# Mixture-of-experts stage: seven of the eight experts in one TensorE loop, fed from a fixed copy of their queue

## What is computed

```python
def _swiglu(x, w1, w3, w2):
    return (jax.nn.silu(x @ w1) * (x @ w3)) @ w2

def _moe(x, w_router, w1, w3, w2):
    logits = (xt @ w_router).astype(jnp.float32)
    top_v, top_e = lax.top_k(logits, TOP_K)          # TOP_K = 2 of N_EXPERTS = 8
    gates = jax.nn.softmax(top_v, axis=-1)
    ...                                              # sort the tokens by expert
    yb = lax.map(run, ...)                           # run: _swiglu(xb, w1[e], w3[e], w2[e])
    y = jnp.zeros((T, D), x.dtype).at[stok].add(yb[dest] * sg[:, None])
```

## Time and profile before

| | us |
|---|---|
| median of 3 runs | 2779.47 (2777.61 to 2779.65) |
| the profiled execution, its own time | 2774.82 |
| its span in the profile | 2773.0 |
| TensorE busy | 2689.7 (97% of the span) |
| experts' up steps, 14336 matmul records | 617.9 busy |
| experts' down steps, 7168 matmul records | 321.1 busy |
| first matmul of expert 0 | at 1828.61 |

### The profile page before, as it was taken

How to read it: one execution, slowest core, us unless ns; L and a number is a source line. 1 busy time by engine, 2 the same in 40 slices (tenths; PEclk the granted TensorE clock), 3 DMA queues, 4 the chain that set the end, 5 groups by cost and what they waited for, 6 DMA issues and landing times.

```text
span 2773.0 us, 73042 instructions
## 1 busy us (share of the span) xinstructions
PE 2689.7 (97%) x33424; PEld 2268.6 (82%) x33424; DVE 890.5 (32%) x1659; ACT 365.2 (13%) x829; POOL 19.6 (1%) x36
## 2 busy tenths in 40 slices
PE   7999999899999999999999999999999999999998
PEld 6877678887667768857877788589999999999997
DVE  5441454623697333444443334410000000000002
ACT  1002241210100023300001242110000000000000
POOL 0000000000000000000000000000000000000000
PEclk9999999999999999999999999999999999999999
DMA  5434232013434434333445242459999999999996
GB/s 198 182 136 184 107 149 85 4 55 137 150 136 158 178 123 152 125 121 139 180 155 196 108 156 107 152 213 391 382 370 398 379 401 373 383 402 373 395 386 256
DMA packets 55718, 601.57 MB, mean 217 GB/s; under 512 B 6337, under 2 KB 6465, under 8 KB 10129
## 3 DMA queue, kind: packets, MB, share of 16 engines
q1 hardware_dynamic: 52272, 587.74, 54.0%
q0 software_dynamic: 3296, 11.57, 1.1%
HBM read 595.48 MB, written 3.81 MB: 216 GB/s over the span
## 4 chain that ended last, share of the span: by engine, by line
PE 91%; DMA 4%; DVE 3%; issue 1%; ACT 1%; POOL 0%; SPq 0%; DVEq 0%; POOLq 0%; ACTq 0%
PE bank L311 21%; PE bank L2511 19%; PE bank L443 10%; PE bank L2523 9%; PE bank L475 8%; PE bank L321 6%; PE bank L464 4%; DMA slot<-in_experts 4%; PE bank L1642 3%; PE bank L1208 2%; PE bank L1628 1%; DVE arena L1833 1%; PE bank L2563 1%; PE bank L936 1%; PE bank L1229 1%
## 5 line engine op out<-in xcount | busy, mean ns | idle before, releaser
L2511 PE MATMUL bank<-arena,slot 128*64 128x96 f32 x14336 | 617.9, 246 | 11.4 <-issue 8.3
L2511 PEld LDWEIGHTS bank<-arena,slot 128*64 128x64 f32 x14336 | 603.2, 137 | 16.3 <-issue 16.0
L311 PE MATMUL bank<-h_cm,slot 128*128 128x256 f32 (+2 forms) x2032 | 448.3, 382 | 1.1 <-ACT h_cm L350 0.5
L311 PEld LDWEIGHTS bank<-h_cm,slot 128*128 128x128 f32 (+2 forms) x2032 | 383.4, 190 | 64.1 <-issue 9.6
L2523 PE MATMUL bank<-ff,slot 128*64 128x96 f32 x7168 | 321.1, 246 | 11.5 <-DMA slot<-in_experts 7.5
L2523 PEld LDWEIGHTS bank<-ff,slot 128*64 128x64 f32 x7168 | 307.7, 137 | 13.7 <-issue 13.6
L2680 DVE TENSOR_TENSOR ff<-ff,bank 128x192 f32<-128x192 f32 x112 | 39.7, 355 | 798.6 <-PE bank L2511 798.6
L475 PE MATMUL bank<-slot,ff 128*128 128x512 f32 x528 | 231.6, 592 | 1.8 <-DVE ff L608 1.8
L475 PEld LDWEIGHTS bank<-slot,ff 128*128 128x128 f32 x528 | 98.7, 190 | 114.6 <-issue 111.9
L464 PE MATMUL bank<-h_cm,slot 128*128 128x256 f32 x704 | 153.6, 379 | 0.4 <-ACT h_cm L352 0.4
L464 PEld LDWEIGHTS bank<-h_cm,slot 128*128 128x128 f32 x704 | 133.7, 190 | 22.5 <-issue 4.9
(11 more groups left out here) (403 smaller groups left out, 2013.9 us busy)
## 6 DMA issues: line engine op xcount, KB each, us to landing
slot<-in_experts SPq DMA_DIRECT2D x112, 2048.0 KB, 9.1
slot<-in_experts SPq DMA_DIRECT2D x112, 1024.0 KB, 9.1
slot<-in_ffn SPq DMA_DIRECT2D x22, 2048.0 KB, 9.3
slot<-in_ffn SPq DMA_DIRECT2D x22, 1024.0 KB, 5.0
slot<-in_dense SPq DMA_DIRECT2D x11, 2048.0 KB, 9.3
slot<-in_dqk SPq DMA_DIRECT2D x8, 2048.0 KB, 8.0
slot<-in_g SPq DMA_DIRECT2D x8, 2048.0 KB, 8.0
slot<-in_w_in_rkv SPq DMA_DIRECT2D x6, 2048.0 KB, 7.7
```

The lines of the kernel that those rows point to most:

```text
L311: ins = pe.matmul(ps[0:m, j * S:(j + 1) * S], w[:, k * width + c0:k * width + c0 + m], rhs[:, k, :], start=k == 0, stop=k == ks - 1)
L2511: ins = pe.matmul(bank[64 * c:64 * c + 64, m * PLACES:(m + 1) * PLACES], slot[s][:, c0:c0 + 64], QUEUE[:, e, k, :], start=k == 0, stop=k = ...
```

## The change

Expert 0 stays written out. Experts 1 to 7 are one engine loop on TensorE with the loop of six rounds inside it. For that, every address in the loop must be the same for each expert: DVE copies the queue of the next expert to a fixed place, CURRENT (128 x 768 f32), and TensorE reads it from there and waits for a new semaphore, current_ready. The sums are always in banks 4 and 5, and the transposes always in 6 and 7. Before down 0 TensorE now waits until banks 4 and 5 have been copied out (sums_read of the expert before), and before the transposes until banks 6 and 7 have been (sums_ready; it has one more count, given once by two tiny copies at the start). ACT, DVE, SP and POOL stay written out as they were.

```diff
+        CURRENT = arena[:, 21248:21248 + KD * PLACES].rearrange("p (k s) -> p k s", s=PLACES)
...
-                                            QUEUE[:, e, k, :], start=k == 0, stop=k == KD - 1, skip_group_check=True)
+                                            CURRENT[:, k, :], start=k == 0, stop=k == KD - 1, skip_group_check=True)
...
-                        ins = pe.matmul(PS[down_bank(e) + d // 4][64 * c:64 * c + 64, (d % 4) * PLACES:(d % 4 + 1) * PLACES],
+                        ins = pe.matmul(PS[4 + d // 4][64 * c:64 * c + 64, (d % 4) * PLACES:(d % 4 + 1) * PLACES],
...
             for half in range(2):
                 pe.wait_ge(sums_read[half], p * N_EXPERTS + e + 1)
+                pe.wait_ge(sums_ready[half], p * (N_EXPERTS + 1) + e + 1)
                 for d in range(4):
-                    ins = pe.transpose(PS[down_bank(e) + half][0:PLACES, d * P:(d + 1) * P], Y_CM[half][:, d, :], ident)
+                    ins = pe.transpose(PS[6 + half][0:PLACES, d * P:(d + 1) * P], Y_CM[half][:, d, :], ident)
...
-                for e in range(N_EXPERTS):
+
+                def expert(e, turn):
                     first = p * ALL_UNITS + e * U_EXPERT + n0
...
+                    pe.wait_ge(named("current_ready"), p * N_EXPERTS + e + 1)
                     up(0, 0)
                     up(0, 1)
-                    if e >= 2:
+                    if turn:
                         for half in range(2):
-                            pe.wait_ge(sums_ready[half], p * N_EXPERTS + e - 1)
+                            pe.wait_ge(sums_read[half], p * N_EXPERTS + e)
                     down(0, 0, start=True)
-                    if e:
+                    if turn:
                         pe_moe_turn(pe, p, e - 1)
                     with pe.Fori(0, U_EXPERT // 2 - 1) as i:
...
+                expert(0, False)
+                with pe.Fori(1, N_EXPERTS) as e:
+                    expert(e, True)
                 pe_moe_turn(pe, p, N_EXPERTS - 1)
...
+                act.copy(stat[:, 13:14], ident[:, 0:1]).then_inc(sums_ready[0], 1)
...
+                def current(e):
+                    if e:
+                        dve.wait_ge(up_ready, p * ALL_UNITS + e * U_EXPERT + n0)
+                    else:
+                        for b in range(2):
+                            dve.wait_ge(named(f"moe_bank_read{b}"), p * moe_reads(b) + moe_reads(b))
+                    v.tensor_copy(CURRENT, QUEUE[:, e]).then_inc(named("current_ready"), 1)
...
+                v.tensor_copy(stat[:, 15:16], ident[:, 0:1]).then_inc(sums_ready[1], 1)
+                current(0)
                 dve.wait_ge(named("places_moved"), p + 1)
                 dve_rows(dve, p)
...
+                    if e < LAST:
+                        current(e + 1)
                     moe_down(dve, p, e, 1, v.tensor_copy)
```

More of the change, by code:

```diff
@@ L2498, in moe_reads, with pe_moe_unit_up @@
             return (GATHERS + TURNED + 1 - b) // 2
-        def pe_moe_unit_up(pe, par, e, n, loads, s):
+        def pe_moe_unit_up(pe, par, n, loads, s):
             pe.wait_ge(slot_loaded[s], 16 * loads)
@@ L2511, in pe_moe_unit_up, with pe_moe_unit_down @@
                             ins = pe.matmul(bank[64 * c:64 * c + 64, m * PLACES:(m + 1) * PLACES], slot[s][:, c0:c0 + 64],
-                                            QUEUE[:, e, k, :], start=k == 0, stop=k == KD - 1, skip_group_check=True)
+                                            CURRENT[:, k, :], start=k == 0, stop=k == KD - 1, skip_group_check=True)
                 ins.then_inc(ready, 1)
-        def pe_moe_unit_down(pe, par, e, n, loads, s, start=False, stop=False):
+        def pe_moe_unit_down(pe, par, n, loads, s, start=False, stop=False):
             pe.wait_ge(slot_loaded[s], 16 * loads)
@@ L2527, in pe_moe_unit_down @@
             ins.then_inc(down_done, 1)
-        def down_bank(e):
-            return 4 + 2 * (e % 2)
         def pe_moe_turn(pe, p, e):
@@ L2577, in up @@
                         at = L + 2 * j
-                        pe_moe_unit_up(pe, (n0 + j) % 2, e, first + j + 2 * i, first_round + (at // SLOTS + 1) + i,
-                                       at % SLOTS)
+                        pe_moe_unit_up(pe, (n0 + j) % 2, first + j + 2 * i, first_round + (at // SLOTS + 1) + i, at % SLOTS)
                     def down(i, j, **kw):
                         at = L + 2 * j + 1
-                        pe_moe_unit_down(pe, (n0 + j) % 2, e, first + j + 2 * i, first_round + (at // SLOTS + 1) + i,
+                        pe_moe_unit_down(pe, (n0 + j) % 2, first + j + 2 * i, first_round + (at // SLOTS + 1) + i,
                                          at % SLOTS, **kw)
+                    pe.wait_ge(named("current_ready"), p * N_EXPERTS + e + 1)
                     up(0, 0)
                     up(0, 1)
-                    if e >= 2:
+                    if turn:
                         for half in range(2):
-                            pe.wait_ge(sums_ready[half], p * N_EXPERTS + e - 1)
+                            pe.wait_ge(sums_read[half], p * N_EXPERTS + e)
                     down(0, 0, start=True)
-                    if e:
+                    if turn:
                         pe_moe_turn(pe, p, e - 1)
@@ L2605, in pe_experts @@
                     if t == 0:
-                        pe.wait_ge(sums_ready[half], p * N_EXPERTS + N_EXPERTS)
+                        pe.wait_ge(sums_ready[half], p * (N_EXPERTS + 1) + N_EXPERTS + 1)
                     pe.matmul(PS[b][:, :], RETURN[:, t * P:(t + 1) * P], SUMS[:, LAST, half * 512:half * 512 + 512],
@@ L2622, in moe_down @@
             eng.wait_ge(down_done, p * ALL_UNITS + e * U_EXPERT + unit_base["experts"] + U_EXPERT)
-            copy(Y_CM[half].rearrange("p d s -> p (d s)"), PS[down_bank(e) + half][:, 0:4 * PLACES]).then_inc(sums_read[half], 1)
+            copy(Y_CM[half].rearrange("p d s -> p (d s)"), PS[4 + half][:, 0:4 * PLACES]).then_inc(sums_read[half], 1)
         def moe_sums(eng, p, e, half, copy):
             eng.wait_ge(sums_turned[half], p * N_EXPERTS + e + 1)
-            copy(SUMS[:, e, half * 512:half * 512 + 512], PS[down_bank(e) + half][0:PLACES, :]).then_inc(sums_ready[half], 1)
+            copy(SUMS[:, e, half * 512:half * 512 + 512], PS[6 + half][0:PLACES, :]).then_inc(sums_ready[half], 1)
         def act_experts(act):
@@ L2753, in pool_experts @@
                     for half in range(2):
-                        pool.wait_ge(sums_ready[half], p * N_EXPERTS + e + 1)
+                        pool.wait_ge(sums_ready[half], p * (N_EXPERTS + 1) + e + 2)
                     pool.sem_inc(named("rows_begun"), 1)
```

## The result

| | median us | runs | ratio of the two, 95% interval |
|---|---|---|---|
| before, on the same chip | 2779.47 | 5, 2777.41 to 2787.2 | |
| changed | 2766.46 | 5, 2763.4 to 2768.42 | 0.995, 0.9933 to 0.9967 |

The change makes the kernel 13.0 us (0.47%) faster. The two profiled executions are 6.4 us apart (2774.82 and 2768.42 us): in them the experts' stage is 10.0 us shorter and starts 3.4 us later.

The account below looks back on a forecast made before the run. TensorE and the weight transfers were both taken to be at their limit, with waits for code and weights at the seams. Gaining 3.0 us and losing 0.8 to the copy gave 2779.47 - 2.2 = 2777.3 us, range 2770 to 2809.

Parts of the forecast that it names:

- What bounds the kernel: Experts' stage: TensorE and transfers both at their limit; stops behind seams are waits for code, 11.0 us in experts 2 to 7.
- The loop stays: Expert loop on TensorE: its code, 6.1 blocks, stays in TensorE's memory, so experts 2 to 7 fetch nothing.
- Rival A: At the loop's branch back, code is gone and fetched again, 3.6 to 12.4 us each; about 2809 us, chance 0.28.
- The ceiling, 9.5 us: Experts 2 to 7: the most the loop could gain, 11.0 us of issue less about 1.5 that stay.
- What is late next. The weights: At expert seams: a fetch wait taken away is mostly paid at the next weight load, leaving 3 us gained.
- The marks it set itself: Signs of being right: 36 packets less, issue under 3 us, weight waits some 10, experts 2 to 5 about 115.
- The copy ahead of expert 0: Before expert 0's first up: DVE's copy to CURRENT delays the whole stage by 0.8 us, between 0.5 and 1.0.
- Later copies, waits, banks: Experts 1 to 7: the seven later copies, the new waits and the fixed banks cost nothing.
- B: Experts' stage: fetches were the bound, the full 9.5 us come back, experts of 113 us; 2770.8 us, chance 0.16.
- C: Experts 2 to 7: weight waits take the whole gain, the copy remains; 2780.3 us, chance 0.56 together with the forecast.

Follow-up runs that it names:

- e1: The changed kernel with the loop over experts 1 to 7 written out again on TensorE: 2777.89 us, ratio to before 0.9996.
- e2: The changed kernel with 24 semaphore increments ahead of the loop, so that it touches one block of code more: 2847.57 us, ratio to before 1.0236.
- e5: The changed kernel with down 13 moved behind the next expert's up 0 and without the copy ahead of expert 0: 2754.7 us, ratio to before 0.9912.
- e6: The kernel before, all experts written out, with down 13 moved behind the next expert's up 0: 2767.12 us, ratio to before 0.9959.
- e7: The kernel before with each weight transfer of the experts cut to a quarter of its columns: 2746.1 us, ratio to before 0.9885.
- e3: The changed kernel with 36 extra 16 KB transfers issued by ACT in experts 2 to 7: 2769.56 us, ratio to before 0.9962.
- e4: The changed kernel with down 13 of an expert moved behind up 0 of the next: 2754.87 us, ratio to before 0.9912.

## Why the prediction was wrong

**What bounds the kernel: right.** Stops behind a seam are TensorE waiting for its code: without the fetches all 9.1 us of them went (11.0 to 1.9), and e1 brought them back.

**The loop stays: right**, by the margin of one block. Rival A had the mechanism right and its price low: 3.6 to 12.4 us a branch, where e2 shows 12.7. Its middle, 36 us for six, was less than half of the 76. The two stops at the branch, 6.43 + 1.79, lie within its range. It left out that the blocks behind them come late in their turn, and that the granted clock falls to 0.50 around such stops. The 7 us of weight waits that it took off were not saved: e2 still has 9.9 us of them in experts 2 to 7.

**The ceiling, 9.5 us: too low.** It took the idle column for what a stop costs. A record lasts 246 ns and the next normally starts 41 ns behind it, so a stop begins before the column counts it. In expert 4 the 32 matmuls from 2309.26 should have taken 1.32 us to the next start, at 2312.17; they took 2.91, a loss of 1.59 where the column says 1.42. Experts 2 to 7 had 22 such waits and have 10: 12 times 0.17 is 2.0 us. With the 5.2 us that the columns show this makes 7.2, and the lower clock takes 1.7 of it back. Measured are 7.0, so some 1.5 us of the gain stand in no wait of the profile and are not explained. For the ceiling itself the same estimate gives 9.1 + 11 x 0.17, or about 11 us. The 1.5 us of waits in expert 7 that stay were 1.9.

**"What is late next. The weights": the step that failed.** It said that a fetch wait taken away is mostly paid at the next load, and kept 3 us of 9.5: 0.2 for each of experts 2 to 6 and 2 for expert 7. The direction was right, the size was not. The marks it set itself were nearly all met (36 packets, issue under 3, weight waits near 10, and experts 2 to 5 near 115 us: 116.2, 114.4, 114.3 and 113.5 against 115.0, 115.1, 115.2 and 114.7). Expert 7 gained its 2.0 us. But experts 2 to 6 gained 5.0 and not 1.0, of which expert 6 alone 3.4 (117.2 to 113.8), so 7.0 us in all where 3 were kept.

Paid back were 3.9 us in waits for weights and 1.7 through the clock, 5.6 of the 9.1 us that issue lost. Against e1 the changed kernel keeps 9.5 us from turn 1 on, and e5 against e6, with the other seam, 9.3, with nothing paid back at a seam. Three things in the argument did not hold:
- It rested on two experts: little fetching and 115.6 us, much fetching and 115.2. In these two both kinds of wait happen to add up to the same, 2.7 and 2.6 us. In experts 2, 3, 5 and 6 of the same trace they add up to 1.8, 2.2, 1.9 and 3.7 (115.0, 115.1, 114.7 and 117.2 us), so the sum is not fixed. At the seams of one kernel the same step waits 0 to 1.92 us before, and 0 to 2.31 after. Two samples of such a spread can't show an exchange of 2 us. Cutting the transfers (e7) asks the question in one run.
- A head start need not last. These are a down load of 2230.54 and the up load 5.3 us behind it, SP's issue to landing, in the changed kernel's expert 3:

```profile
DMA to landing us min/median/max: 7.6/7.6/7.6
...
DMA to landing us min/median/max: 10.2/10.2/10.2
```

  No code was fetched between them, and the next seam waited 1.82 us (at 2287.88). What the transfers had won before such a slow spell seems to be gone at the seam, whatever TensorE did behind the last one; this is read from one place and not tested.
- It held the transfers' times fixed. Behind the seams the loads land 1.2 us sooner without fetches (the rows at e3).

**The copy ahead of expert 0, 0.8 us (0.5 to 1.0): right.** 1.44 - 0.74 = 0.70 us, and 0.71 by e5. The rest of the later start (1832.04 against 1828.61) arose in code ahead that is the same in both; such starts differ by 5.2 us between e4 and the changed kernel. Part of it is the clock again: ahead of this point the changed kernel's trace has four stretches at 0.50, that of before three and that of e4 two.

**Later copies, waits, banks at nothing: right.** No wait for DVE's copy in experts 1 to 7, and e1 equals before.

**The rivals.** B (2770.8, the fetches were the bound, "experts of 113 us") came nearest, with 0.16, though 4.3 us too slow. Its full 9.5 us back agree with the 8.6 to 11.2 us by which the stage shrank (e5 against e6, the changed kernel against e1). With the old seam this agreement is partly luck: there 5.6 us did come back, and a ceiling that was too low by about 1.5 us and the unexplained gain make up for part of it. C is refuted. The medians say 13.0 us with an interval from about 9 to 19, the stage 10.0; expert 1, which still fetches, was 2.7 us shorter in the changed kernel's trace from turn to turn, and that is not explained by the loop. So the 10.8 us between the forecast and the median are not all this step: on the profiled executions, to which its sum belongs (2772.6 against 2768.42 us), it was off by 4.2.

## What to carry to other kernels

Where an engine waits for two things in turn, don't conclude from one trace that they exchange: remove each by itself, or cut the crowded one to a quarter, and add up. A loop on TensorE that must not be fetched again has a size and a place: count the blocks that it touches, with one more for what is fetched ahead, since one block too many cost 81 us here, six times what the loop brought. The best version has both edits, 24 to 26 us (0.9%) under before; its stage is 10 to 11 us above that with a quarter of the weights. And read the granted clock beside the stops: a stop can cost time behind it that no wait shows.

## What was not expected of the hardware

- TensorE keeps eight blocks of 16 KB, by e2 and the changed kernel. One more, and a loop does not lose one block but all nine, at 12.7 us a round (q8: 91 packets, then 145).
- The granted clock fell to 0.50 behind stops: behind a wait for weights of 2.31 us, but not behind waits of 2.06 and 1.82 us in the same trace, and around every branch back of e2. It cost 1.7 us of the stage in the changed kernel and 16 in e2.
- The same 16 KB fetch is hidden at a DMA share of 0.35 and makes TensorE wait up to 1.6 us at 0.95 (e1). Behind the branch of e2 the wait is up to 7.3 us, though the transfers of weights run dry there.
- The order at the seam is worth as much as the loop: one down step of 2.8 us moved behind an up step of 5.3 took 10 us out of the stage.
